# Column matmuls, an earlier load of the state-space inputs, and the tap transposes behind the small vectors' copy

## The chip, the cores and the metric

The kernel runs on one core of one Trainium2 chip. The metric is the device time of one execution in microseconds (us), as the median of several runs. Engines are named as in the profile: PE is TensorE's matmul side, PEld its weight loads, DVE is VectorE, ACT is ScalarE, POOL is GpSimd, SP is SyncE (here it only issues DMAs).

## The reference

Two residual layers over 256 tokens of width 1024, all float32. Each layer computes six conditioning vectors from one vector `c`, and uses them as shift, scale and gate of its two sub-layers:

```
mod = (c_act @ w_mod[l] + b_mod[l])        # 6 * 1024 values, six vectors
sh1, sc1, g1, sh2, sc2, g2 = split(mod, 6)
h = rmsnorm(x, norm1_g[l]) * (1 + sc1) + sh1
proj = h @ w_in[l]                          # q k v | conv a b | ssm u | gates
mixed = gate_a * attention + gate_c * conv + gate_s * ssm
x = x + g1 * (mixed @ w_out[l])
h2 = rmsnorm(x, norm2_g[l]) * (1 + sc2) + sh2
x = x + g2 * ((silu(gate) * up) @ w_ffn_out[l])
```

The state-space (ssm) branch needs small tables made from `ssm_b_*` (2 x 128 KB a layer) and `ssm_c_*` (2 x 128 KB a layer). The convolution branch needs 31 taps for each of 512 channels.

## The kernel before, in words

Every large weight block is 1 MB and goes through one of four buffers `raw`. SP loads it; ACT rounds it to a high part `whi` (line 1018); DVE subtracts to get the low part `wlo` (line 1363); PE then runs three matmuls for each product (lines 547 to 549: high x high, high x low, low x high). The blocks follow one fixed list of names: `su` 0 and 1, `q` 0 and 1, `kv`, and so on, then the gates, `wo`, and at the end of a layer the feed-forward blocks `fg`, `fu`, `fo`. Each engine runs its own program in that order, so an engine that waits holds up all that stands behind it in its program. Small work (rotations, attention, ssm, convolution) is set between the blocks at numbered places.

The conditioning product runs beside the blocks in pieces `mod` (line 583), three groups `ng` of 2048 values a layer, so six groups in all. The sum lies in PSUM bank `b_mod` as four rows, at partitions 0, 32, 64 and 96, of 512 values each; the other partitions hold copies and unused rows. DVE adds the bias into `modrow` (line 1517, 128 x 512). PE then brings the values into columns in `mod_columns` (line 591): it transposes all of `modrow` in four pieces of 128 x 128, and DVE copies out the 16 columns that matter with a stride (`mod_vectors`, line 1505). Group 0 of layer 0 is needed by the first norm (line 1540); the others are made ahead, among the blocks.

SP's program is the list `ITEMS` of `mod` and `main` blocks, each with a wait until its `raw` buffer is free, with other loads set between. `load_c` issues the two `ssm_c` loads into `uc` (line 441), `load_b` the two `ssm_b` loads into `yc` (line 437). In layer 0 they stand before the block `("main", 0, 2)`, which is `q` 0; `("main", 0, 1)` is `su` 1. The users of `uc` are a POOL copy (line 988) and then the transposes of `prep_round` on PE (line 769); the user of `yc` is `b_source` on DVE (line 1456).

The small per-channel vectors of a layer (norm gains, biases, ssm parameters) land as rows in `prod` and are transposed by PE into bank `b_y` (`small_columns`, lines 869 and 870); DVE copies them to `vec` and `ldv` (lines 1761 and 1762), whose end is the semaphore `vec_cp`. The taps are transposed into other columns of the same bank (`tap_columns`, line 879) and copied to `tapv` (line 1767). For layer 1 both happen in layer 0 between the blocks `fg` 0 and `fu` 0.

Of the kernel before, what the change touches and what calls it, by code (L numbers as in the profile page):

```python
# [30 lines left out]
P = 128  # L31
# [150 lines left out]
def lo_engine(i):  # L182

    return "dve"
# [70 lines left out]
def trunk(nc, A, out):  # L255
    with ExitStack() as ctx:
        def sb(name, shape, dt=F32):
            return ctx.enter_context(nc.sbuf_tensor(name, shape, dt))

        def sem(name):  # L260
            return ctx.enter_context(nc.semaphore(name))

        bank = [ctx.enter_context(nc.psum_tensor(f"bank{n}", [P, 512], F32)) for n in range(8)]
        b_mod, b_y = bank[2], bank[3]
# [38 lines left out]
        modrow = sb("modrow", [P, 512])  # L303
# [3 lines left out]
        ident = sb("ident", [P, P])  # L307
        ones = sb("ones", [P, P])
        rot = sb("rot", [P, P])
        consts = sb("consts", [P, 16])  # L310
# [10 lines left out]
        modv = sb("modv", [P, 48])  # L321
# [40 lines left out]
        b_ready, cc_ready, c_twice, tap_tr, tap_cp = sem("b_ready"), sem("cc_ready"), sem("c_twice"), sem("tap_tr"), sem("tap_cp")  # L362
# [8 lines left out]
        ldt_spread, vec_tr, vec_cp, c_tr, silu_c, c_ready = (  # L371
            sem(n) for n in "ldt_spread vec_tr vec_cp c_tr silu_c c_ready".split())
        row_zero, s_bias, mod_row, mod_tr, mod_ready, scale_ready, g_tr, g_ready = (
            sem(n) for n in "row_zero bias_landed mod_row mod_tr mod_ready scale_ready g_tr g_ready".split())
# [28 lines left out]
        def landed_in(item):  # L403

            return raw[SLOT[item]][:, :], s_land[SLOT[item]], LANDED[item]
# [17 lines left out]
        def small_vectors(eng, l):  # L423

            for r0, n, name in ((R_N1, 8, "norm1_g"), (R_N2, 8, "norm2_g"), (R_DWB, 4, "conv_dw_b"),
                                (R_LNG, 4, "conv_ln_g"), (R_LNB, 4, "conv_ln_b"), (R_D, 4, "ssm_d")):
                eng.dma_start(rows[r0:r0 + n, :], A[name][l].rearrange("(r c) -> r c", c=P)).then_inc(s_rows[l], 16)
            for r0, name in ((R_ARE, "ssm_a_re"), (R_AIM, "ssm_a_im")):
                eng.dma_start(rows[r0:r0 + ST, :], A[name][l].rearrange("(s g) n -> s (g n)", g=2)).then_inc(s_rows[l], 16)
            eng.dma_start(ldt[:, :], A["ssm_log_dt"][l].rearrange("(s g) -> s g", g=2)).then_inc(s_rows[l], 16)  # L430

        def load_taps(eng, l):
            eng.dma_start(taps, A["conv_dw_w"][l]).then_inc(s_taps[l], 16)

        def load_b(eng, l):
            for c, name in enumerate(("ssm_b_re", "ssm_b_im")):
                eng.dma_start(bn[:, c], A[name][l].rearrange("g n i -> (g n) i").rearrange("(s p) i -> p s i", p=P)).then_inc(s_b[l], 16)

        def load_c(eng, l):
            for c, name in enumerate(("ssm_c_re", "ssm_c_im")):  # L440
                eng.dma_start(csrc[:, c, :, 0:HEAD], A[name][l].rearrange("g o n -> (g o) n").rearrange("(s p) n -> p s n", p=P)).then_inc(s_cc[l], 16)

        def load_x(eng):
            for j in range(2):
                eng.dma_start(x[:, j, :], A["x"][0, j * P:(j + 1) * P, :]).then_inc(s_x, 16)

        def load_bias(eng, l, ng):
            eng.dma_start(modrow[0:P:32, :],
                          A["b_mod"][l, ng * MODC:(ng + 1) * MODC].rearrange("(q n) -> q n", q=4)).then_inc(s_bias, 16)

        def late_constants(eng):
            eng.dma_start(rot[:, :], A["c_rot"]).then_inc(s_const2, 16)
            eng.dma_start(posi, A["positions"].to_broadcast([P, T])).then_inc(s_const2, 16)
            eng.dma_start(sink[:, :, :], A["attn_sinks"].rearrange("(o l) q -> o l q", o=1).to_broadcast([P, DEPTH, NQ])).then_inc(s_const2, 16)

        @block.sync
        def _(sp):
# [33 lines left out]
            for item in ITEMS:  # L491
                if item == ITEMS[1]:
                    load_x(sp)
                if item == ("main", 0, 2):
                    load_c(sp, 0)
                    load_b(sp, 0)
                if item == ("main", 0, 3):
                    late_constants(sp)
                was = AFTER.get(item)
                if was and was[0] == "main":  # L500

                    e = lo_engine(was[2])
                    sp.wait_ge(s_lo[e], LO_NO[(was[1], was[2])] + 1)
                elif was:

                    sp.wait_ge(s_modused, MOD_NO[was] + 1)
                dst, landed, _ = landed_in(item)
                if item[0] == "mod":
                    _, l, ng, k = item
                    if k == 4 and (l, ng) != (0, 0):  # L510

                        sp.wait_ge(mod_tr, 3 * l + ng)
                        if ng != 1:
                            sp.wait_ge(g_tr, 4 * l + (2 if ng == 2 else 0))
                        load_bias(sp, l, ng)
                    sp.dma_start(dst, A["w_mod"][l, k * P:(k + 1) * P, ng * MODC:(ng + 1) * MODC]).then_inc(landed, 16)
                else:
                    if item[1:] == (0, AT[("gc", 3)]) and DEPTH > 1:

                        sp.wait_ge(gl_read, 4)  # L520
                        small_vectors(sp, 1)
                        load_taps(sp, 1)
                    for d, src in main(item[1], item[2], dst):
                        sp.dma_start(d, src).then_inc(landed, 16)
                    if item[1] == 0 and DEPTH > 1 and item[2] == AT[("fg", 0)]:

                        sp.wait_ge(c_lo, 1)
                        load_c(sp, 1)
                        load_b(sp, 1)
                    if item[1:] == (DEPTH - 1, AT[("fg", 0)]):  # L530

                        sp.wait_ge(s_ready, 2 * DEPTH)
                        sp.dma_start(final_g, A["final_norm_g"].rearrange("(o n) -> o n", o=1).to_broadcast([P, D])).then_inc(s_final_g, 16)
            for n in range(4):
                j, c = divmod(n, 2)
# [7 lines left out]
        def _(pe):  # L543
            mm = nc.tensor.matmul
# [42 lines left out]
            def mod_columns(n):  # L587

                pe.wait_ge(mod_row, n + 1)
                for j in range(4):  # L590
                    last = nc.tensor.transpose(b_mod[:, j * P:(j + 1) * P], modrow[:, j * P:(j + 1) * P], ident[:, :])
                last.then_inc(mod_tr, 1)

            def g_rows(l, ng, half):
# [278 lines left out]
            def tap_columns(l):  # L873

                pe.wait_ge(s_taps[l], 16)
                if l == 0:
                    pe.wait_ge(vec_cp, 1)
                for c in range(CT):
                    last = nc.tensor.transpose(b_y[:, 256 + c * 32:256 + c * 32 + TAPS], taps[:, c * P:(c + 1) * P], ident[0:TAPS, 0:TAPS])
                last.then_inc(tap_tr, 1)  # L880
# [41 lines left out]
            for k in range(DK):  # L922
# [10 lines left out]
                if k == 3:  # L933
                    tap_columns(0)
            mod_columns(0)

            def behind_norm(l, i):
# [395 lines left out]
        def _(dve):  # L1333
            step = Steps(s_dve)
            V = nc.vector
# [164 lines left out]
            def mod_vectors(l, ng):  # L1500

                n = 3 * l + ng
                dve.wait_ge(mod_tr, n + 1)
                c0 = 16 * ng
                V.tensor_copy(modv[:, c0:c0 + 16].rearrange("p (q j) -> p j q", q=4), b_mod[:, :].rearrange("p (j r) -> p j r", j=4)[:, :, 0:P:32]).then_inc(mod_ready, 1)
                dve.wait_ge(mod_ready, n + 1)
                if ng != 1:
                    s, m0, r0 = (scale1, M_SC1, R_N1) if ng == 0 else (scale2, M_SC2, R_N2)
                    V.scalar_tensor_tensor(out=s[:, :], in0=modv[:, m0:m0 + DK], scalar=1.0, in1=vec[l][:, r0:r0 + DK], op0=ALU.add,
                                           op1=ALU.mult).then_inc(scale_ready, 1)  # L1510
                    dve.wait_ge(scale_ready, 2 * l + (ng == 2) + 1)
# [244 lines left out]
            def small_vectors_in(l):  # L1756

                dve.wait_ge(vec_tr, l + 1)
                if l:
                    dve.wait_ge(tap_tr, l + 1)  # L1760
                V.tensor_copy(vec[l][:, :], b_y[:, 0:VROWS])
                V.tensor_copy(ldv[l][:, :], b_y[:, P:P + ST]).then_inc(vec_cp, 1)

# [64 lines left out]
            lo(0)  # L1828
            mod_bias(0)
            mod_vectors(0, 0)  # L1830
            norm(0, "su", 0, scale1, M_SH1)
            lo(1)
            b_source(0, 0)
            for l in range(DEPTH):
                for i in range(NB):
                    for n in mod_ends_at(l, i - 2):
                        mod_vectors(*divmod(n, 3))
# [88 lines left out]
```

## Time and profile before

| what | value |
|---|---|
| three runs | 1014.95, 1015.76 and 1019.72 us; median 1015.76 us |
| profiled execution, its own time | 1014.95 us |
| its span, first to last instruction | 1013.1 us |
| mean granted TensorE clock | 0.972 of full speed |
| PE busy, DVE busy, ACT busy | 937.6, 669.5, 469.1 us |

The profiled execution is the fastest of the three and lies 0.81 us under the median. What lies outside its span is 1.85 us. The granted clock has two levels, 1.00 (2.4 GHz) and 0.50 (1.2 GHz); a value between them in a row is a stretch that holds some of both.

### The profile page before, as it was taken

Reading aid. Unit: us, or ns where it says so; the run is one execution under the profiler, and the core shown is the slowest. Engines: PE = TensorE matmul, PEld = TensorE weight load, DVE = VectorE, ACT = ScalarE, POOL = GpSimd, SP = SyncE. Lnnn points to the kernel's source line nnn. Section 1 sums busy time; section 2 is a strip of 40 time slices with the busy share of each in tenths; the row PEclk is TensorE's granted clock in tenths of the full one; section 3 lists DMA queues with packets and bytes.
Section 4 is the critical chain, followed back from the end, with each engine's and each line's share of the span. In section 5 each row is a group of like instructions: output and inputs, shape, how many; then the busy total and the mean of one; then the engine's idle time right before and its main releaser. Section 6 shows DMA issues by size and latency. Waiting matters only on the chain.

```text
span 1013.1 us, 16086 instructions
## 1 busy us (share of the span) xinstructions
PE 937.6 (93%) x6839; PEld 785.3 (78%) x6839; DVE 669.5 (66%) x913; ACT 469.1 (46%) x548; POOL 9.3 (1%) x11
## 2 busy tenths in 40 slices
PE   5689998999999999999997998999999899999995
PEld 2488885666766979889996997666676699999994
DVE  3773977999477673565456576899966655454445
ACT  4485135623645664545345323574264454343342
POOL 2000000000000000000000000000000000000000
PEclk9799999999999999999998999999999989999998
DMA  9965235548767555565657335454967545565621
GB/s 345 227 214 209 85 126 208 206 133 285 263 246 192 184 180 208 208 209 208 225 191 166 126 126 197 153 207 151 275 231 281 190 133 201 170 204 169 203 87 41
DMA packets 128023, 194.01 MB, mean 192 GB/s; under 512 B 30706, under 2 KB 90618, under 8 KB 121808
## 3 DMA queue, kind: packets, MB, share of 16 engines
q1 hardware_dynamic: 127608, 192.85, 56.9%
q8 instruction: 54, 0.88, 0.4%
q10 hardware_dynamic: 344, 0.14, 0.1%
q14 instruction: 17, 0.14, 0.0%
HBM read 191.93 MB, written 1.05 MB: 190 GB/s over the span
## 4 chain that ended last, share of the span: by engine, by line
PE 64%; DVE 23%; DMA 5%; ACT 4%; issue 3%; ACTq 1%; DVEq 0%
PE bank L547 18%; PE bank L548 18%; PE bank L549 18%; DVE wlo L1363 7%; DVE yc L1648 7%; PE bank L583 2%; DMA prod<-in_conv_dw_w 2%; PE bank L648 2%; ACT whi L1018 1%; PE bank L671 1%; DMA raw<-in_w_in 1%; DMA raw<-in_w_out 1%; PE bank L659 1%; DMA raw<-in_w_mod 1%; PE bank L769 1%
## 5 line engine op out<-in xcount | busy, mean ns | idle before, releaser
L1363 DVE TENSOR_TENSOR wlo<-raw,whi 128x2048 fp32r<-128x2048 f32 (+1 forms) x135 | 302.7, 2243 | 234.7 <-PE bank L549 191.9
L1018 ACT ACTIVATE whi<-raw 128x2048 fp32r<-128x2048 f32 x132 | 252.3, 1912 | 159.7 <-DMA raw<-in_w_in 75.4
L547 PE MATMUL bank<-hhi,whi 128*128 128x256 f32 x992 | 289.3, 292 | 11.8 <-DVE hlo L1545 9.3
L548 PE MATMUL bank<-hlo,whi 128*128 128x256 f32 x992 | 285.2, 287 | 0.0
L549 PE MATMUL bank<-hhi,wlo 128*128 128x256 f32 x992 | 284.8, 287 | 0.0
L547 PEld LDWEIGHTS bank<-hhi,whi 128*128 128x128 f32 x992 | 195.0, 197 | 21.0 <-issue 16.2
L548 PEld LDWEIGHTS bank<-hlo,whi 128*128 128x128 f32 x992 | 195.1, 197 | 0.6
L549 PEld LDWEIGHTS bank<-hhi,wlo 128*128 128x128 f32 x992 | 194.9, 196 | 0.0
L547 PE MATMUL bank<-whi,bhi 128*128 128x512 f32 x304 | 121.4, 399 | 3.4 <-DVE wlo L1363 3.4
L548 PE MATMUL bank<-wlo,bhi 128*128 128x512 f32 x304 | 119.1, 392 | 0.0
L549 PE MATMUL bank<-whi,blo 128*128 128x512 f32 x304 | 118.7, 391 | 0.0
L547 PE MATMUL bank<-whi,hhi 128*128 128x512 f32 x256 | 105.5, 412 | 2.4 <-DVE wlo L1363 2.2
L549 PE MATMUL bank<-whi,hlo 128*128 128x512 f32 x256 | 100.4, 392 | 0.0
L548 PE MATMUL bank<-wlo,hhi 128*128 128x512 f32 x256 | 100.4, 392 | 0.0
L1648 DVE SCALAR_TENSOR_TENSOR yc<-uc,tapv,yc 128x256 f32<-128x256 f32 x240 | 97.3, 479 | 0.1
L547 PEld LDWEIGHTS bank<-whi,bhi 128*128 128x128 f32 x304 | 57.4, 189 | 21.3 <-issue 5.3
L1238 ACT ACTIVATE bhi<-gate 128x512 fp32r<-128x512 f32 x22 | 13.9, 632 | 124.5 <-DVE gate L1722 124.5
L547 PEld LDWEIGHTS bank<-whi,hhi 128*128 128x128 f32 x256 | 48.4, 189 | 26.0 <-issue 11.7
L583 PE MATMUL bank<-raw,cact 128*32 128x512 f32 x384 | 54.9, 650 | 13.8 <-DMA raw<-in_w_mod 9.5
L549 PEld LDWEIGHTS bank<-whi,blo 128*128 128x128 f32 x304 | 57.3, 189 | 12.5
L548 PEld LDWEIGHTS bank<-wlo,bhi 128*128 128x128 f32 x304 | 57.5, 189 | 10.6
L549 PEld LDWEIGHTS bank<-whi,hlo 128*128 128x128 f32 x256 | 48.3, 189 | 10.7
(250 smaller groups left out, 818.0 us busy)
## 6 DMA issues: line engine op xcount, KB each, us to landing
raw<-in_w_mod SPq DMA_DIRECT2D x48, 1024.0 KB, 7.2
raw<-in_w_ffn_in SPq DMA_DIRECT2D x44, 1024.0 KB, 5.1
raw<-in_w_in SPq DMA_DIRECT2D x38, 1024.0 KB, 5.3
raw<-in_w_ffn_out SPq DMA_DIRECT2D x22, 1024.0 KB, 5.0
raw<-in_w_out SPq DMA_DIRECT2D x8, 1024.0 KB, 6.1
raw<-in_w_in SPq DMA_DIRECT2D x16, 256.0 KB, 4.9
raw<-in_ssm_glu_b SPq DMA_DIRECT2D x4, 1024.0 KB, 5.1
raw<-in_ssm_glu_a SPq DMA_DIRECT2D x4, 1024.0 KB, 5.1
```

The source lines that it names most:

```text
L547: mm(o, w_hi, a_hi, start=start, stop=False, skip_group_check=True)
L548: mm(o, w_hi, a_lo, start=False, stop=False, skip_group_check=True)
L549: return mm(o, w_lo, a_hi, start=False, stop=stop, skip_group_check=True)
L583: last = mm(b_mod[32 * q:32 * q + 32, :], cact32[:, k, :], weights[:, q * 512:(q + 1) * 512], start=(k == 0), stop=(k == DK - 1), skip_gro ...
L648: last = mm(o, bl[r, a, STEPS - 1 - j, k, :], u_ssm[r, k, j * NC:(j + 1) * NC], start=(k == 0 and a == 0 and j == 0), stop=(j == STEPS - 1 ...
L659: mm(o[:, t * NC:T], kf[:, k, t, :], u_ssm[:, k, 0:(STEPS - t) * NC], start=(k % 2 == 0 and t == 0), stop=False, skip_group_check=True)
L671: last = mm(b_out[k // 2][r:r + 32, c0 + 1:c0 + NC], ca[:, a, j, 4 * k + 2 * half + q, :], s[:, a, q, k, 0:NC - 1], start=False, stop=(a = ...
L769: last = nc.tensor.transpose(round_bank(l, n)[:, k * P:(k + 1) * P], src, ident[:, :])
L1018: fn(whi[mi % N_HI][:, :], raw[SLOT[item]][:, :], ACT.Copy).then_inc(s_hi, 1)
L1238: fn(bhi[:, a:a + 2, :], gate[:, a:a + 2, :], ACT.Copy).then_inc(act_hi, 1)
L1363: part = V.tensor_tensor(wlo[mi % N_LO][:, n], raw[SLOT[("main", *divmod(mi, NB))]][:, n], whi[mi % N_HI][:, n].bitcast(F32), ALU.subtract)
L1648: last = V.scalar_tensor_tensor(out=yc[:, c, :], in0=uc[:, c, k:k + T], scalar=w, in1=yc[:, c, :], op0=ALU.mult, op1=ALU.add)
```

## The change

It has three parts.

1. In layer 0, SP issues the two `ssm_c` and the two `ssm_b` loads one block earlier: before `su` 1, no longer before `q` 0.
2. `mod_columns` no longer transposes `modrow`. Each of its four pieces is the stationary operand of a float32 matmul whose moving operand is `consts[:, 0:4]`, four columns that hold a 1 at partition 0, 32, 64 or 96. Each gives 128 x 4 values, side by side in the first 16 columns of `b_mod`, and DVE copies these 16.
3. In layer 1's tap transposes, PE first waits for DVE's copy of the small vectors (`vec_cp`, as layer 0's do already), and DVE's copy no longer waits for the tap transposes (`tap_tr`).

```
-                if item == ("main", 0, 2):
+                if item == ("main", 0, 1):
                     load_c(sp, 0)
                     load_b(sp, 0)
...
                 for j in range(4):
-                    last = nc.tensor.transpose(b_mod[:, j * P:(j + 1) * P], modrow[:, j * P:(j + 1) * P], ident[:, :])
+                    last = mm(b_mod[:, 4 * j:4 * j + 4], modrow[:, j * P:(j + 1) * P], consts[:, 0:4], start=(j == 0), stop=(j == 3), skip_group_check=True)
                 last.then_inc(mod_tr, 1)
...
                 pe.wait_ge(s_taps[l], 16)
-                if l == 0:
-                    pe.wait_ge(vec_cp, 1)
+                pe.wait_ge(vec_cp, l + 1)
...
-                V.tensor_copy(modv[:, c0:c0 + 16].rearrange("p (q j) -> p j q", q=4), b_mod[:, :].rearrange("p (j r) -> p j r", j=4)[:, :, 0:P:32]).then_inc(mod_ready, 1)
+                V.tensor_copy(modv[:, c0:c0 + 16].rearrange("p (q j) -> p j q", q=4), b_mod[:, 0:16].rearrange("p (j q) -> p j q", q=4)).then_inc(mod_ready, 1)
...
                 dve.wait_ge(vec_tr, l + 1)
-                if l:
-                    dve.wait_ge(tap_tr, l + 1)
                 V.tensor_copy(vec[l][:, :], b_y[:, 0:VROWS])
```

## Rows read from the trace of the kernel before

**Rows 1.** The page: busy time by engine, and the chain's shares.

```profile
PE 937.6 (93%) x6839; PEld 785.3 (78%) x6839; DVE 669.5 (66%) x913; ACT 469.1 (46%) x548; POOL 9.3 (1%) x11
...
PE 64%; DVE 23%; DMA 5%; ACT 4%; issue 3%; ACTq 1%; DVEq 0%
```

**Rows 2.** The chain, 36 to 48 us: start, length, what.

```profile
36.45 1.13 PE bank L591 x4
...
40.63 1.80 ACT whi L1018
...
44.94 2.20 DVE wlo L1363
47.14 1.14 DVE gate L1456
```

**Rows 3.** Timeline of SP's DMA issues, 22 to 40 us: start, length.

```profile
26.45 0.38 SPq L524 DMA_DIRECT2D raw<-in_w_in  x1
...
27.50 3.76 SPq L441 DMA_DIRECT2D uc<-in_ssm_c_im  x1
...
33.71 3.46 SPq L437 DMA_DIRECT2D yc<-in_ssm_b_im  x1
```

**Rows 4.** Tile raw, issues at 26 to 27 us; tile yc, 20 to 60 us.

```profile
DMA to landing us min/median/max: 10.2/10.2/10.2
...
DMA to landing us min/median/max: 6.3/6.6/6.9
```

**Rows 5.** Timeline of POOL, ACT and PE, the loads' users, 37 to 49 us.

```profile
37.37 0.61 POOL L988 COPY uc<-uc 128x512 f32<-128x512 f32 x1 [12.44 <-DMA uc<-in_ssm_c_im]
...
45.66 1.92 ACT L1018 ACTIVATE whi<-raw 128x2048 fp32r<-128x2048 f32 x1 [1.37 <-DMA raw<-in_w_in]
...
47.77 1.03 PE L769 MATMUL bank<-ident,uc 128*128 128x128 f32 x8
```

**Rows 6.** Timeline of PE, PEld and DVE: column transposes, and loads before short matmuls.

```profile
36.45 1.11 PE L591 MATMUL bank<-ident,modrow 128*128 128x128 f32 x4 [0.89 <-DVE modrow L1517]
37.60 0.19 DVE L1505 COPY modv<-bank 128x16 f32<-128x16 f32 x1 [1.21 <-PE bank L591]
...
84.05 0.16 PEld L782 LDWEIGHTS bank<-prod,decay 128*32 128x32 f32 x7
...
122.91 0.42 PEld L659 LDWEIGHTS bank<-u_ssm,kf 128*128 128x128 f32 x3
```

**Rows 7.** Line 659 by shape: count | busy us, mean ns | idle.

```profile
L659 PEld LDWEIGHTS bank<-u_ssm,kf 128*128 128x128 f32 x64 | 9.5, 191 | 0.5
```

**Rows 8.** The chain at two later groups.

```profile
206.05 0.48 DVE yc L1648
...
304.88 0.44 PE bank L591 x4
```

**Rows 9.** Timeline of DVE, PE and PEld, 332 to 339 us.

```profile
332.04 2.29 DVE L1363 TENSOR_TENSOR wlo<-raw,whi 128x2048 fp32r<-128x2048 f32 x1 [1.78 <-PE bank L549]
332.12 0.32 PEld L879 LDWEIGHTS bank<-ident,prod 31*128 31x128 f32 x4
332.48 0.39 PE L547 MATMUL bank<-hhi,whi 128*128 128x256 f32 x1
...
334.38 0.16 DVE L1762 COPY ldv<-bank 128x16 f32<-128x16 f32 x1
...
338.60 2.29 DVE L1363 TENSOR_TENSOR wlo<-raw,whi 128x2048 fp32r<-128x2048 f32 x1 [3.86 <-PE bank L549]
```

**Rows 10.** Windows of PE: length, busy (count), granted clock, DMA share, GB/s.

```profile
60.00:66.00 6.00, 4.67 (x27) 0.72 0.53 184
324.00:330.00 6.00, 4.33 (x34) 1.00 1.10 377
```

**Rows 11.** Waits of PE, 59 to 61.5 us and 323 to 326 us: total, times, longest.

```profile
PE bank L769 <- ACT blx L1082: 2.1, 1, 2.1
...
PE bank L547 <- DVE hlo L1545: 2.3, 1, 2.3
```

## The prediction

> **What bounds the kernel now.** I read the page first: PE is busy for 93% of the span, and the chain that ended last is 64% PE and 23% DVE [rows 1]. A microsecond of PE is therefore worth a microsecond only where the chain runs on PE, and each edit has to be placed in the chain first. I then read the chain piece by piece around each edited line, the timeline of the engines there, and the windows with the granted clock.
>
> The first norm is where part 1 and part 2 meet. The chain goes from the landing of the last `mod` weights over the four column transposes to DVE's norm, then through ACT's rounding of `su` 1 at 40.63, DVE's `wlo` at 44.94 and `b_source` at 47.14 [rows 2]. Here PE is no bound; the queue of ACT and DVE is.
>
> **Part 1, the earlier loads.** Who waits for `ssm_c` and `ssm_b`? POOL's copy starts at 37.37, as `ssm_c` lands, but PE uses its result only at 47.77 [rows 5]. The second `ssm_b` load was issued at 33.71 and landed 6.3 to 6.9 us later [rows 3, 4], so by 40.6 at the latest, while DVE comes to it at 47.14 straight from its own work [rows 2]. Nobody on the chain waits for either, so landing earlier gains nothing. One load behind them gains: `q` 0 is waited for by ACT, 1.37 us until 45.66 [rows 5], but the chain between 44.94 and 50 runs on DVE, so this is worth nothing as well.
>
> What it costs is the load that is moved past. `su` 1 is issued at 26.45 and lands 10.2 us later, at 36.7 [rows 3, 4]; ACT takes it up at about 40.6 [rows 2], so it has 3.9 us of slack. After the change it stands behind four issues that took SP from 26.87 to 37.17 [rows 3]. They can start about 1.2 us earlier, since SP need not wait for `su` 1's buffer first, which puts the issue of `su` 1 at about 36.0. The two long issue times look like SP waiting for room in the queue (the one of 3.76 us ends at 31.3, that of 3.46 at 37.2, where 0.38 us do for a 1 MB load), and with `su` 1 no longer ahead of them the room may come sooner; 34.5 is the early end. A 1 MB load in a queue with nothing ahead takes about 5 us: estimate of the landing 39.5 to 41.2. ACT wants it at 40.6, or 0.85 later by part 2. So the price is 0, with 0.6 us as the upper end if part 2 turns out free. I take 0.
>
> **Part 2, the columns.** Before: four transposes. After: four float32 matmuls with the same stationary 128 x 128 and 4 moving columns in place of 128. A float32 matmul that is no transpose has two loads and two matmuls in the trace (line 659 has 64 loads in two layers for 32 calls [rows 7]), a transpose one of each. So 4 loads become 8, while the moving part shrinks to nothing.
>
> What does a load cost when nothing long covers it? The nearest row is that of float32 loads 128 x 128 ahead of 64-column matmuls: three of them take 0.42 us, the last one 0.19, so they start 0.115 apart; I use 0.11 [rows 6]. Eight of them: 0.88 us. The four transposes take 0.44 us of the chain at full clock [rows 8]. That is +0.44 us of PE for each group. The bounds: the 32-column loads that go into different quarters of the array start about 0.01 to 0.02 apart (seven in 0.16 us, the last 0.11 of it) [rows 6]; at that price a group would gain 0.3 us. If loads and matmuls didn't overlap at all, 8 x 0.16 = 1.3 us, +0.85. I take the 128 x 128 row, which is the same shape and type.
>
> The Trainium skill ("TensorE: Matmul & The Clock Gate", Back-to-back issue gap) gives an isolated matmul of 1 to 64 columns a floor of about 25 ns; eight of them would be 0.2 us, and a group would then gain 0.24 us. The row of line 659 speaks against it, since there the load and not the matmul sets the pace.
>
> Now the six groups one by one. The first one runs at the granted clock of 0.50 and is wholly on the chain: the copy starts 1.15 us after the first transpose [rows 6]. At half clock the loads start 0.22 apart: 8 x 0.22 = 1.76, and the last short matmul ends about 0.21 later (a transposed 128-column piece lasts 0.42 there, of which 0.21 is streaming). Copy after 2.0 us: +0.85. The groups at 205 and 691 us lie where the chain is DVE's convolution [rows 8]: 0. Those at 304.9, 495.0 and 791.1 lie on PE's chain, with the same row three times [rows 8]: 3 x 0.44 = +1.32. DVE's copy reads 16 values a partition either way: 0. Sum of part 2: +2.2 us, between -1.6 and +4.
>
> **Part 3, the taps of layer 1.** DVE's dropped wait is worth nothing: its copies come at 334.25, directly behind the `wlo` that it started at 332.04, and the tap transposes were over by 332.5 [rows 9]. The new wait of PE is another matter. PE finishes `fg` 0 at 331.9, does the small transposes, goes on to the taps at 332.12 and begins `fu` 0 at 332.48. The copy that it now waits for ends at 334.54 [rows 9], since DVE does 2.29 us of `wlo` first. PE would then start the tap transposes at 334.60 and `fu` 0 0.36 us later, at 334.96: 2.48 us late. What stands behind it in PE's queue is the block `fu` 0, and DVE waits for its end: 3.86 us idle until 338.60 [rows 9]. There is no slack on that side, ACT waits in turn for DVE, and SP's loads hang on DVE; so the whole 2.48 us goes into the end. Bounds 2.3 and 2.6. POOL's clearing of `prod` comes later too and has no one waiting.
>
> **The clock behind that stall.** PE will do nothing but four tiny transposes between 332.1 and 335.0. After the wait of 2.13 us that ended at 61.33 the granted clock fell to its lower level and came back: 0.72 over the 6 us from 60, so 1.7 us lost [rows 10, 11]. After the wait of 2.3 us that ended at 325.67 it stayed 1.00 [rows 10, 11]. Both happen after stalls of this length. Mine is a little longer than both, so I take the drop as somewhat likelier than not: +1.7 us, bound below 0, above 3.4 (two such stretches).
>
> **The sum.** 0 + 2.2 + 2.5 + 1.7 = +6.4 us on the profiled execution's own 1014.95 us: 1021.3 us, 0.63% more. Without the clock drop it is +4.7, 1019.6 us, 0.46%. The median of the runs shown is 0.8 us above that execution, and one run of three was 4.8 us above it. The measurement of this kernel tells about 0.5%, 5 us, from no change, so the two cases lie on either side of that line.
>
> **The rivals.**
> *The clock stays up.* The same sum without the drop: the stall falls as the one at 325 did. 1019.6 us, within 0.5%. This is the mechanism that puts the result on the other side; its place is the stretch from 335 to 339 us, and it decides from 1.3 us on (6.4 - 5.1). For it speaks the window from 324, against it that from 60 [rows 10].
> *The matmul sets the pace, not the load.* Then a group costs no more than before, or gains 0.24 to 0.3 us on the chain three times and 0.5 at the start. Sum -1.3 + 2.5, and +1.7 with the drop: 1016.2 to 1017.9 us; at price nothing 1017.4 to 1019.1. The Trainium skill's floor of 25 ns, on the page named above, would lead here. Against it stands the spacing of 0.11.
> *`su` 1 comes late.* If the four small loads hold SP up for longer than before, `su` 1 lands at 43 or 44, ACT's queue with the second half of the norm stands behind it, and 2 to 3 us come on top: 1022 to 1024.5 us. Against it: those four issues took 10.3 us in all while 3 MB were queued ahead, and now less is.
> *PE's stall is taken up later*, by a wait that shrinks. It would need a releaser that doesn't hang on `fu` 0, which I find none of up to 362 us. 1018 us.
>
> **How the numbers follow.** Forecast with the drop 0.38; the clock stays up 0.27; the matmul sets the pace 0.15, half of it with the drop; `su` 1 late 0.10; taken up 0.05; something else that makes it faster 0.05. The range 1016.5 to 1024.0 takes in all but the outermost of them. Slower by over 0.5%: the forecast mostly, the late `su` 1 and a fifth of the rival without the drop, 0.49; faster 0.04; within, the rest, 0.47.
>
> **What would show each step.** Right: two PE records for each of four calls at line 591, eight loads about 0.11 apart at full clock and 0.22 at the start, and the first copy of `modv` 2.0 us after the first of them; a wait of PE at line 879 of about 2.4 us, released by DVE's line 1762, and `fu` 0 about 2.5 us later behind `fg` 0's end; a clock under 1.00 right behind it. ACT's rounding of `su` 1 without a wait for a DMA. Wrong: loads closer than 0.08 at line 591; ACT idle for `in_w_in` before its second rounding; no PE wait at line 879, or PE's later waits shorter by as much. The total would go wrong most easily by the clock's drops elsewhere, each worth 1.7 to 3.4 us, which a shift of a microsecond can add or take away.

## The result, and the profile after

| | before | after |
|---|---|---|
| median of 6 executions each, side by side on one chip | 1018.59 us (1014.95 to 1020.23) | 1025.16 us (1022.23 to 1026.0) |
| ratio, with its 95% interval | | 1.007 [1.0051, 1.0091] |
| profiled execution, its span | 1014.95, 1013.1 us | 1024.41, 1022.6 us |
| mean granted clock in it | 0.972 | 0.966 |

The changed kernel is slower by 0.7% by the ratio, by 6.6 us (0.64%) by the medians, where the forecast's sum was 6.4 us. The forecast time of 1021.3 us was still missed, and so was its range's upper end of 1024.0, since the kernel before itself has a median of 1018.59 us in this comparison and the sum stood on an execution of 1014.95. Three of the six executions of the kernel before are those that the prediction had; the three new ones took 1018.01, 1019.16 and 1020.23 us. Of all executions in this document one, of e1_loads, was in a slow state (1323.99 us at a mean clock of 0.65) and is left out of its median and ratio.

Of the page after, busy time and the chain's shares, which answer to [rows 1]:

```profile
PE 945.4 (92%) x6863; PEld 792.6 (78%) x6863; DVE 669.6 (65%) x913; ACT 469.1 (46%) x548; POOL 8.7 (1%) x11
...
PE 63%; DVE 23%; DMA 5%; ACT 5%; issue 3%; ACTq 1%; DVEq 0%
```

There are 24 more records on PE, as six groups of eight in place of four need. The other engines work as long as before. In the changed kernel, lines from 876 on stand one lower than before up to about 1500, and three lower behind the dropped wait.

The first norm, timeline after, beside [rows 2, 6]:

```profile
36.18 1.78 PEld L591 LDWEIGHTS bank<-consts,modrow 128*128 128x128 f32 x8 [2.62 <-DVE modrow L1516]
36.18 1.87 PE L591 MATMUL bank<-consts,modrow 128*128 128x4 f32 x8 [0.89 <-DVE modrow L1516]
38.09 0.18 DVE L1504 COPY modv<-bank 128x16 f32<-128x16 f32 x1 [1.96 <-PE bank L591]
```

Eight weight loads (LDWEIGHTS, side PEld) take 1.78 us at the lower clock, 0.22 each, and the copy starts 1.91 us behind the first matmul; it was 1.15. The chain after, at the three groups that lie on PE (each stood at 0.44, one of them in [rows 8]):

```profile
306.43 0.79 PE bank L591 x8
...
502.35 0.79 PE bank L591 x8
...
800.04 0.79 PE bank L591 x8
```

That is +0.35 us each, 0.10 us for one load and matmul. The Trainium skill ("TensorE: Matmul & The Clock Gate", LDWEIGHTS (loading the stationary operand)) gives a load its number of columns divided by 1.2, in ns: 107 ns for 128, an estimate of 0.85 us for eight. The trace roughly agrees at the higher clock, with 0.79; at the lower one it has 1.78, twice that, so the one figure does not hold for both. Its floor of 25 ns for a short matmul (same page, Back-to-back issue gap) is no use here, since the loads set the pace.

SP's issues after, beside [rows 3], and the users of the loads, POOL and ACT, beside [rows 5]:

```profile
25.62 0.43 SPq L441 DMA_DIRECT2D uc<-in_ssm_c_re  x1
26.10 0.51 SPq L441 DMA_DIRECT2D uc<-in_ssm_c_im  x1
26.65 3.47 SPq L437 DMA_DIRECT2D yc<-in_ssm_b_re  x1
30.16 3.72 SPq L437 DMA_DIRECT2D yc<-in_ssm_b_im  x1
33.93 7.34 SPq L524 DMA_DIRECT2D raw<-in_w_in  x5
```

```profile
34.10 0.61 POOL L987 COPY uc<-uc 128x512 f32<-128x512 f32 x1 [8.82 <-DMA uc<-in_ssm_c_im]
```

```profile
41.02 1.89 ACT L1017 ACTIVATE whi<-raw 128x2048 fp32r<-128x2048 f32 x1
```

`su` 1 is issued at 33.93, 7.5 us later than before, lands 6.5 us on, at 40.4, and ACT rounds it at 41.02 without having waited for it. `ssm_c` is there 3.3 us earlier for POOL, and nothing comes of that.

The taps, timeline after of PE and then of DVE, beside [rows 9]:

```profile
334.87 0.28 PE L549 MATMUL bank<-hhi,wlo 128*128 128x256 f32 x1
...
337.91 0.60 PE L878 MATMUL bank<-ident,prod 31*128 31x31 f32 x4 [2.40 <-DVE ldv L1759]
338.44 0.58 PE L547 MATMUL bank<-hhi,whi 128*128 128x256 f32 x1
```

```profile
335.26 2.29 DVE L1362 TENSOR_TENSOR wlo<-raw,whi 128x2048 fp32r<-128x2048 f32 x1 [2.99 <-PE bank L549]
337.47 0.21 DVE L1758 COPY vec<-bank 128x64 f32<-128x64 f32 x1
337.60 0.16 DVE L1759 COPY ldv<-bank 128x16 f32<-128x16 f32 x1
338.55 0.29 DVE L1764 COPY tapv<-bank 128x124 f32<-128x124 f32 x1 [0.79 <-PE bank L878]
345.79 2.29 DVE L1362 TENSOR_TENSOR wlo<-raw,whi 128x2048 fp32r<-128x2048 f32 x1 [6.96 <-PE bank L549]
```

PE waits 2.40 us for two small copies that stand behind DVE's `wlo` of 2.29 us. From one `wlo` to the next it was 6.56 us (332.04 to 338.60), and it is now 10.53: +3.97. The windows after show what is not the wait itself. Their columns are the length, the busy time (and count) of PE, PEld, DVE, ACT and POOL, the granted clock, the DMA share and GB/s; all windows below have the same:

```profile
336.00:338.00 2.00, 0.09 (x1) 0.12 (x2) 1.76 (x3) 1.58 (x1) 0.00 (x0) 0.96 0.00 0
338.00:340.00 2.00, 2.00 (x11) 1.94 (x12) 0.29 (x1) 0.00 (x0) 1.36 (x2) 0.50 0.57 176
340.00:342.00 2.00, 2.00 (x14) 2.00 (x14) 0.00 (x0) 0.00 (x0) 0.14 (x1) 0.68 1.00 347
```

PE did almost nothing from 336 to 338, and from 338 to 340 the granted clock was at its lower level (0.50, 1.2 GHz), where a 256-column matmul lasts 0.41 us in place of 0.28. The 3.97 us are 2.5 of waiting (e5 below measures it alone) and 1.5 of the clock.

### The profile page after: what moved, and what is told of

The parts are those of the page before. It is cut to its first block, busy times and chain, and to the rows that moved or that the text cites. A ratio compares the mean times of both kernels' runs of the same rounds, so it can differ in the third digit from the quotient of the medians.

```text
span 1022.6 us, 16134 instructions
## 1 busy us (share of the span) xinstructions
PE 945.4 (92%) x6863; PEld 792.6 (78%) x6863; DVE 669.6 (65%) x913; ACT 469.1 (46%) x548; POOL 8.7 (1%) x11
## 3 DMA queue, kind: packets, MB, share of 16 engines
HBM read 191.93 MB, written 1.05 MB: 189 GB/s over the span
## 4 chain that ended last, share of the span: by engine, by line
PE 63%; DVE 23%; DMA 5%; ACT 5%; issue 3%; ACTq 1%; DVEq 0%
PE bank L547 18%; PE bank L548 17%; PE bank L549 17%; DVE wlo L1362 7%; DVE yc L1647 7%; PE bank L583 2%; DMA prod<-in_conv_dw_w 2%; PE bank L648 2%; ACT whi L1017 2%; DMA raw<-in_w_in 2%; PE bank L671 1%; DMA raw<-in_w_out 1%; PE bank L659 1%; DMA raw<-in_w_mod 1%; PE bank L747 1%
## 6 DMA issues: line engine op xcount, KB each, us to landing
raw<-in_w_mod SPq DMA_DIRECT2D x48, 1024.0 KB, 7.2
raw<-in_w_ffn_in SPq DMA_DIRECT2D x44, 1024.0 KB, 5.1
raw<-in_w_in SPq DMA_DIRECT2D x38, 1024.0 KB, 5.5
raw<-in_w_ffn_out SPq DMA_DIRECT2D x22, 1024.0 KB, 5.0
raw<-in_w_out SPq DMA_DIRECT2D x8, 1024.0 KB, 6.2
raw<-in_ssm_glu_b SPq DMA_DIRECT2D x4, 1024.0 KB, 5.1
raw<-in_ssm_glu_a SPq DMA_DIRECT2D x4, 1024.0 KB, 5.1
```

## The experiments

Each ratio is to the kernel before, run beside it on the same chip, with a 95% interval. e8 has one execution, the profiled one.

**One part at a time.** Four kernels made from the one before: part 1 alone, part 2 alone, part 3 alone, and parts 1 and 2 together (each with its lines of the diff shown above).

e1_loads, the first hunk alone. 

> Part 1 alone: the four ssm loads of layer 0 one block earlier. My reading (nobody on the chain waits for them, and su 1 still lands before ACT takes it up): 0 us, ratio 0.9995 to 1.0005 apart from the scatter of the runs. If the loads are what gains or costs: the rival 'su 1 late' wants +2 to +3 us, ratio 1.002 to 1.003, with ACT idle for in_w_in ahead of its second rounding; a gain would need b_source or the transposes of ssm_c to start earlier.

e2_columns, the second and fourth hunk alone. 

> Part 2 alone: column matmuls in place of the transposes. Loads set the pace: +0.76 us at the first group (as the changed kernel shows) and +0.44 at each of the three groups on PE's chain, together +2.1 us, ratio 1.002; PE records at line 591 start 0.11 apart at full clock. The matmul sets the pace (the rival): the groups at full clock gain 0.24 to 0.3 us each, sum -0.1 us, ratio 1.000.

e3_taps, the third and fifth hunk alone. 

> Part 3 alone: layer 1's tap transposes wait for DVE's copy. The stall goes into the end in full: +2.5 us, and +1.7 us more in the executions where the clock falls behind it, so +2.5 to +4.2 us, ratio 1.0025 to 1.0041. The rival that the stall is taken up later: under +1 us, ratio under 1.001, with the same delay seen at fu 0 and gone at the end of layer 0.

e4_no_taps, the first, second and fourth. 

> Parts 1 and 2 without part 3. If the parts add up: +2.1 us, ratio 1.002, that is the changed kernel less 2.5 to 4.2 us. If part 3 isn't the larger part of the loss, this is near the changed kernel, ratio 1.005 or more.

| kernel | median, beside a before of 1014.64 us | ratio |
|---|---|---|
| e1_loads | 1013.93 | 1.000 [0.9986, 1.0014] |
| e2_columns | 1016.95 | 1.0022 [1.0003, 1.0041] |
| e3_taps | 1018.5 | 1.0045 [1.0027, 1.0063] |
| e4_no_taps | 1016.66 | 1.0023 [1.0004, 1.0041] |

The parts add up: 0 + 0.22 + 0.45 = 0.67%, where the whole change has 0.7. The earlier loads are worth nothing alone and nothing on top of part 2. Each interval is some 0.2% wide to either side, so the sum is good to no more than that. Part 3 alone costs more in its own trace than in the changed kernel's; its windows say why:

```profile
334.00:337.00 3.00, 3.00 (x15) 2.94 (x16) 0.29 (x1) 0.00 (x0) 1.51 (x2) 0.50 0.77 242
337.00:340.00 3.00, 3.00 (x16) 3.00 (x15) 0.00 (x0) 0.00 (x0) 0.00 (x0) 0.50 0.31 108
```

The wait is again 2.4 us, but the clock stays low for all of these 6 us. From `wlo` to `wlo` it is 11.95 us here (331.32 to 343.27), +5.39: 2.5 of waiting and 2.9 of the clock. The whole kernel has only 3.9 us more in its median, so an execution does not always lose that much.

**The stall with the clock held.** Part 3, with five matmuls of no use (their result is overwritten) between `fg` 0's end and the wait:

```
+                if l:
+                    for n in range(5):
+                        mm(bank[4 + n % 4][:, 0:T], ones[:, :], x[:, 0, 0:T], start=True, stop=True, skip_group_check=True)
                 pe.wait_ge(vec_cp, l + 1)
```

e5_taps_filled. 

> Part 3 alone, but PE runs five float32 matmuls of 256 columns, whose result nobody reads, on the bank that fo 0 clears later, in front of the wait for DVE's copy (2.15 us at 0.43 each). This separates the stall from the clock: the wait for the copy stays, but PE isn't idle. If the clock behind the stall is the rest of part 3's 4.6 us: the clock stays at 1.00 behind it, fu 0 is 2.5 us late and no more, +2.5 us, ratio 1.0025. If the 4.6 us have another cause, for instance DVE's changed order: ratio 1.0045 as before. If DVE's copy itself comes later, more.

Measured: 1018.23 us beside 1016.2, ratio 1.0016 [1.0004, 1.0027]. The timeline of its PE and DVE:

```profile
334.00 2.43 PE L878 MATMUL bank<-x,ones 128*128 128x256 f32 x10
336.38 0.43 PE L881 MATMUL bank<-ident,prod 31*128 31x31 f32 x4
```

```profile
333.82 2.29 DVE L1365 TENSOR_TENSOR wlo<-raw,whi 128x2048 fp32r<-128x2048 f32 x1 [2.99 <-PE bank L549]
...
342.87 2.29 DVE L1365 TENSOR_TENSOR wlo<-raw,whi 128x2048 fp32r<-128x2048 f32 x1 [5.73 <-PE bank L549]
```

The filler takes the place of the wait (0.35 us of which is left), so `fu` 0 is as late as the wait alone would make it: from `wlo` to `wlo` 9.05 us, +2.49, the wait's own length. The clock is 1.00 all through, and nothing else is lost:

```profile
334.00:337.00 3.00, 3.00 (x17) 2.40 (x17) 2.48 (x4) 2.15 (x2) 0.06 (x1) 1.00 0.08 31
337.00:340.00 3.00, 3.00 (x27) 3.00 (x27) 0.14 (x1) 0.00 (x0) 1.45 (x2) 1.00 0.89 290
```

Against e3, 0.29% or 2.9 us is gone, as much as the clock took in e3's trace. So the stall's price has two terms, the wait and the clock behind it. The traces show both; the ratios fit, but the shifts below move a ratio by as much, so they alone would not show it.

**The stall taken away.** Part 3, with the tap transposes and their copy one block later on both engines, when `vec_cp` is long done:

```
                         small_columns(l + 1)
-                        tap_columns(l + 1)
+                    if i == PREP_AT and l + 1 < DEPTH:
+                        tap_columns(l + 1)
```

e6_taps_later. 

> Part 3 alone, with layer 1's tap transposes and their copy set one block later (ahead of fg 1, not fu 0), where DVE's copy of the small vectors is long done. If the wait for the copy is the whole cost: fu 0 follows fg 0 without a stall, ratio 1.000 (within 0.0015). If anything else of part 3 costs: up to 1.0045.

Measured: 1016.95 us beside 1016.2, 0.9998 [0.9982, 1.0013]. DVE's timeline:

```profile
334.68 2.29 DVE L1363 TENSOR_TENSOR wlo<-raw,whi 128x2048 fp32r<-128x2048 f32 x1 [2.99 <-PE bank L549]
...
340.99 2.29 DVE L1363 TENSOR_TENSOR wlo<-raw,whi 128x2048 fp32r<-128x2048 f32 x1 [3.81 <-PE bank L549]
```

6.31 us from `wlo` to `wlo` (without the tap transposes, which now come later), and no cost. The order of the waits is harmless; what costs is where the wait stands in PE's queue.

**Load or matmul?** The kernel before, with float32 matmuls of 64 moving columns in place of its transposes (DVE's copy takes the 16 columns out with a stride, as before):

```
+                    last = mm(b_mod[:, 64 * j:64 * j + 64], modrow[:, j * P:(j + 1) * P], ident[:, 0:P:2], start=(j == 0), stop=(j == 3), skip_group_check=True)
```

e8_columns64. 

> The kernel before with column matmuls of 64 moving columns (every second column of the identity) in place of 4. Loads set the pace: the eight records of a group start 0.11 apart at full clock as with 4 columns, and a group on PE's chain costs the same 0.88 us. The matmul sets the pace: with 64 columns a group takes clearly longer than with 4, by up to 8 x 0.05 = 0.4 us.

Measured: 1019.62 us, one execution. Its chain at the same three groups, all alike:

```profile
306.40 0.84 PE bank L591 x8
```

Sixteen times the columns of part 2 (0.79) add 0.05 us to eight matmuls, so the moving columns don't set the pace; what stays is the load.

**A shift alone.** The clock drops at different places in each of these traces, so I asked what a mere shift does. The kernel before, with tiny transposes of `crow` in PE's first wait, while it waits for the first loads; nothing of theirs is used:

```
+            for _ in range(30):
+                nc.tensor.transpose(b_y[:, 0:DK], crow[:, :], ident[0:DK, 0:DK])
             for k in range(DK):
                 mod_block(0, 0, k)
```

e12_shifted. 

> The kernel before with 30 transposes of c's 8 rows, nobody's input, in PE's first wait (3.8 to 8.1 us), which covers them. They add as many PE instructions as the fillers of the start do (60 records) and touch neither a wait nor the clock of any later stretch. If the place of the instructions in PE's program costs by itself (PE's waits that the trace calls issue grow or new ones come, 1.9 us at 95 us before, 2.3 to 2.7 us in the kernels with more PE instructions): ratio 1.001 to 1.004, and issue waits of 1 to 2.7 us at other places. If the fillers' loss has another cause: 1.000.

Measured: 1020.94 us beside 1016.7, 1.0048 [1.0031, 1.0065]. That is as much as part 3 has, with no wait and no work added on any path. Four others follow it: 10 and 60 in the kernel before, and 10 and 30 in the changed kernel.

e14_shift10. 

> The kernel before with 10 tiny transposes of crow in PE's first wait (20 more records on PE's side), nothing else. Theory A (the position of PE's instructions sets where its waits for nothing visible fall, and what they cost): another set of such waits than with 30, and a ratio anywhere between 0.998 and 1.006. Theory B (a time rises with the number of added instructions, 60 records for +0.48%): +0.16%, ratio 1.0016. Theory C (run e12 fell by chance into another state of the clock): ratio 1.000.

e15_shift60. 

> The same with 60 tiny transposes (120 more records). They may reach past PE's first wait by at most 1 us at its start. Theory A: a ratio between 0.998 and 1.006 without relation to the count. Theory B: +0.96%, ratio 1.0096. Theory C: 1.000 to 1.001.

e16_after10. 

> The changed kernel with 10 tiny transposes in PE's first wait. If its +0.7% is all its own waits and loads (0.76 us at the start, 3 x 0.35, 2.5 of the stall and the clock behind it, 5.8 in sum), ratio 1.0055 to 1.009 as before. If the position of instructions has a share in it, the ratio moves by up to 0.4% either way: 1.003 to 1.011.

e17_after30. 

> The changed kernel with 30 tiny transposes in PE's first wait. If the shift's +0.48% of the kernel before is a price that adds, ratio 1.0115. If it is a matter of position, anywhere from 1.003 to 1.011. If the changed kernel's cost is its own and the shift costs nothing here, 1.007.

| transposes added | kernel before | changed kernel |
|---|---|---|
| 0 | 1 | 1.007 [1.0051, 1.0091] |
| 10 | 1.0013 [1.0001, 1.0025] | 1.011 [1.0092, 1.0129] |
| 30 | 1.0048 [1.0031, 1.0065] | 1.0074 [1.0057, 1.0091] |
| 60 | 1.0059 [1.0041, 1.0077] | not run |

A price that adds for each instruction would put 60 at 1.0096 and the changed kernel with 30 at 1.012; both lie outside the intervals. What is left is that something which depends on the position of PE's instructions matters, by up to 0.6% in the kernel before and 0.4% in the changed one. One place shows how it may. It is a wait of PE for nothing that the profile sees ("issue"). All of them in the view of PE's waits, over the whole execution, first before, then e12:

```profile
PE bank L648 <- issue: 1.9, 1, 1.9
```

```profile
PE bank L648 <- issue: 2.7, 1, 2.7
PE bank L547 <- issue: 2.1, 1, 2.1
PE bank L548 <- issue: 0.8, 1, 0.8
```

The second is new, stands in the middle of a block at 471 us, and the lower clock follows it, as the windows of e12 and then of before show:

```profile
470.00:472.50 2.50, 1.01 (x9) 0.81 (x7) 0.00 (x0) 2.36 (x2) 0.00 (x0) 1.00 0.97 376
472.50:476.00 3.50, 2.87 (x16) 2.88 (x17) 0.00 (x0) 0.00 (x0) 0.00 (x0) 0.68 0.11 36
```

```profile
470.00:472.50 2.50, 2.50 (x18) 2.28 (x18) 0.98 (x1) 0.00 (x0) 0.00 (x0) 1.00 0.17 66
472.50:476.00 3.50, 3.50 (x17) 2.91 (x16) 2.80 (x4) 1.55 (x2) 0.00 (x0) 1.00 0.21 58
```

In e15 a wait of 2.1 us of that kind stands at line 549, in e14 only the one at line 648 has grown, to 2.8. Two executions of one kernel, e9 and e13 below, have nearly the same such waits (2.5 and 0.6 us, 2.4 and 0.4), so they seem to belong to the program. That PE's instructions come too late there is my guess; no run tells what the engine waits for.

The clock is another matter. The changed kernel and the one before have the same wait of PE for ACT, here in the timeline of each, before and then after:

```profile
417.06 0.63 PE L769 MATMUL bank<-ident,ca 128*128 128x128 f32 x4 [2.15 <-ACT blx L1082]
```

```profile
422.78 0.71 PE L769 MATMUL bank<-ident,ca 128*128 128x128 f32 x4 [2.15 <-ACT blx L1081]
```

Windows of 5 us ahead of the end of that wait and behind it, again before and then after:

```profile
412.00:417.00 5.00, 2.92 (x14) 2.08 (x12) 0.53 (x1) 4.85 (x5) 0.00 (x0) 1.00 0.65 261
417.00:422.00 5.00, 4.94 (x31) 4.46 (x32) 3.19 (x4) 2.60 (x3) 0.00 (x0) 1.00 0.42 128
```

```profile
417.70:422.70 5.00, 2.94 (x14) 2.10 (x12) 0.51 (x1) 4.87 (x5) 0.00 (x0) 1.00 0.66 265
422.70:427.70 5.00, 4.92 (x17) 4.05 (x18) 3.07 (x3) 2.58 (x3) 0.00 (x0) 0.66 0.39 126
```

Up to the end of the wait PE does the same work in the same pattern, 14 matmuls in 2.9 us of 5; behind it the clock is 1.00 in one kernel and 0.66 in the other, 1.7 us lost (0.34 x 5). It comes 5.7 us later in the changed kernel, but that is not what decides. e9 and e13 below are one kernel, profiled twice. Each has the same wait (2.14 us, at 412.60 and 413.81), and behind it the windows of e9 and then of e13 are:

```profile
412.54:417.54 5.00, 4.94 (x18) 4.02 (x19) 3.06 (x3) 2.60 (x3) 0.00 (x0) 0.66 0.41 129
```

```profile
413.75:418.75 5.00, 4.94 (x31) 4.49 (x32) 3.19 (x4) 2.61 (x3) 0.00 (x0) 1.00 0.40 127
```

So the same wait of the same program costs a stretch of low clock in one execution and none in another. Over the 18 traces it does in 8, and their times do not sort them: with the wait's end at 418.00 us (e6) the clock stays up, at 418.11 (e4) it falls, at 418.46 (e14) it stays up. The wait of 2.33 us for `hlo`, after which the clock stayed up in [rows 10, 11], is such another: of the 15 traces that have it unfilled, the clock fell behind it in 10, e1's among them (0.58 over 6 us), which has no change near it. A single trace therefore doesn't say whether a wait of this length will cost its clock, and the difference between two traces is in part the luck of the execution.

**Filling waits on purpose.** If a low clock costs, keeping PE busy in its unavoidable waits should pay. The kernel before, with matmuls of no use ahead of a block whose input is late: e9 at the start, before the first ssm rounds and around the norms of both layers; e10 at the start and before those rounds alone; e11 around the norms alone. e9 and e10 also have one more wait of PE at the start, for the copy of the taps (`tap_cp`), since these fillers write where the taps lie.

```
+            def fill(o, n, src):
+                for _ in range(n):
+                    mm(o, ones[:, :], src, start=True, stop=True, skip_group_check=True)
...
                     o = unit_bank(l, i)
+                    fill(o[:, 0:T], 5 if l or kind == "fg" else 3, cosr[:, :] if l or kind == "fg" else x[:, 0, 0:T])
...
+                if k >= 5:
+                    fill(b_y[:, 0:T], {5: 8, 6: 2, 7: 1}[k], x[:, 0, 0:T])
```

e9_fill. 

> The kernel before, with matmuls that nobody reads in PE's waits: eleven among the first mod pieces, four before the transposes at 61 us, three to five before the norm's first product, five among the transposes of the second layer's first norm. If the granted clock falls because of PE's waits and its fall is on the chain: the first group's work and the stretches behind 61, 543 and 809 us run at the higher clock, -5 to -8 us, ratio 0.992 to 0.995. If the lower clock there lies beside other work, or the fillers get in the way: 0.998 to 1.002.

e10_fill_start. 

> Only the fillers of the first 62 us: eleven matmuls among the last three mod pieces of layer 0's first group, four before the transposes at 61 us. If the clock at the start is what the filled kernel gains by: the first group's last piece and its transposes run at 1.00 (about -1.5 us up to the first norm) and the stretch behind 61 us too (-1.5 us), ratio about 0.997. If it is all in the later norms: 1.000.

e11_fill_norms. 

> Only the fillers before the first product of each norm (three in the first, five in the others) and the five among the transposes of the second layer's first norm. The stretches behind 543 and 809 us stay at 1.00: 6.8 us at half speed each in the kernel before, of which 3.4 us each would be lost, if all of it were on the chain. Ratio 0.995 to 0.998. With the start alone as the cause: 1.000.

e13_fill_again, e9's kernel again, on another occasion. 

> The filled kernel once more, beside other kernels and on whatever chip comes. Its two halves alone gave 1.0029 and 0.9978, together 0.9943. If 0.9943 stands it is within 0.992 to 0.996 again; if its halves simply add up, it is near 1.0007.

| kernel | median, and before beside it | ratio |
|---|---|---|
| e9_fill | 1010.94, 1016.2 | 0.9943 [0.9926, 0.996] |
| e13_fill_again | 1010.29, 1016.7 | 0.994 [0.9918, 0.9962] |
| e10_fill_start | 1020.74, 1017.04 | 1.0029 [1.0013, 1.0045] |
| e11_fill_norms | 1015.59, 1017.04 | 0.9978 [0.9959, 0.9998] |

All fillers together beat both kernels, twice. Windows of e9, then of before, at the start:

```profile
26.00:36.00 10.00, 8.51 (x47) 4.87 (x44) 4.86 (x13) 2.95 (x3) 0.00 (x0) 1.00 1.02 314
36.00:60.00 24.00, 20.57 (x153) 18.89 (x152) 22.18 (x32) 18.86 (x27) 0.61 (x1) 1.00 1.01 241
```

```profile
26.00:36.00 10.00, 4.10 (x20) 0.36 (x16) 4.68 (x14) 3.11 (x3) 0.00 (x0) 0.75 0.99 312
36.00:60.00 24.00, 19.77 (x140) 18.99 (x140) 21.20 (x29) 17.44 (x25) 0.61 (x1) 0.82 0.92 233
```

The halves do not add up: e10 is slower. One place where it gives back is the stretch from 92 us, with before under it:

```profile
92.00:106.00 14.00, 11.50 (x149) 11.38 (x150) 4.19 (x7) 1.91 (x1) 0.00 (x0) 0.53 0.37 143
```

```profile
92.00:106.00 14.00, 12.08 (x244) 11.83 (x240) 4.57 (x9) 2.48 (x2) 0.00 (x0) 0.76 0.60 223
```

A clock of 0.53 in place of 0.76 for 14 us is 3.2 us of full speed (0.23 x 14). This is one execution of each, and such a stretch differs between executions too (0.76 in e9, 0.88 in e13). The medians do say that e10 is slower and e9 faster, beyond their intervals; why e10 loses is open, position among the candidates. Of e9's 0.6%, the part that belongs to the fillers themselves stays open by as much as the shifts above are worth.

## Why the prediction was wrong, point by point

**The failing step** is the first sentence of the sum: "0 + 2.2 + 2.5 + 1.7 = +6.4 us on the profiled execution's own 1014.95 us: 1021.3 us". The difference held, the level under it didn't. The six executions of the kernel before that stood beside the changed one have a median of 1018.59 us, 3.6 us above that anchor; on it the same sum gives 1025.0 us, against 1025.16 measured. The prediction said that one run of three was 4.8 us above the anchor, and then let the range's upper end, 1024.0, follow from the rivals' prices alone. The lowest of three executions is not the level of the next ones. Beside the other experiments the kernel before had medians from 1014.64 to 1017.04, so the level itself is uncertain by some 4 us.

**Part 1: 0, right.** e1 measures 1.000. The estimate of `su` 1's issue (34.5 to 36.0) was a little late, 33.93; it landed at 40.4, in the estimated range, and ACT was ready for it only at 41.02. The long issues stayed long: 3.47 and 3.72 us for `ssm_b` re and im, where before `ssm_c` im had 3.76, `ssm_b` re 2.37 and `ssm_b` im 3.46. With `su` 1 no longer ahead, SP is held up one load later, and the four take 8.3 us in place of 10.3 (25.62 to 33.88). Room did come sooner. The rival of a late `su` 1 is out in the trace and by e1.

**Part 2: +2.2, the mechanism right, each term a little large.** At the start +0.76 against +0.85, on PE's chain 3 x 0.35 against 3 x 0.44, so 1.8 us in all. The groups under DVE's convolution have no piece at line 591 in the chain, as said. e2 and e4 measure 2.2 and 2.3 thousandths, but a shift of 10 transposes alone has 1.3, so their size confirms nothing finer than the sign. The rival in which the matmul sets the pace is out: e8, with 16 times the columns, has 0.84 against 0.79.

**Part 3, the wait: +2.5, right.** 2.40 us at line 878, released by the copy, and with the clock held (e5) the step from `wlo` to `wlo` is longer by 2.49. No later wait took it up: from the `wlo` behind the stall to the last one it is 649.02 us in e3's trace (343.27 to 992.29) and 649.33 in e1's (340.43 to 989.76), which has no stall. e3's +3.9 us in the whole time fits, and that rival is out too. e6 shows, to within 0.2%, that the cost is the wait's place alone.

**The clock behind it: +1.7, right in the changed kernel (1.5), 2.9 in e3, bounds 0 and 3.4 kept.** The rival in which the clock stays up, which had 0.27, did not come in any trace where PE is left idle: in e3, the changed kernel and the two shifted ones a window behind the stall has 0.50 to 0.53, and the step from `wlo` to `wlo` is 11.95, 10.53, 10.57 and 11.87 us. Four of four is not proof that it always falls. The row that spoke for this rival, 1.00 behind the wait at 325 us, was the rarer case of its own wait (5 of 15 traces). e5 is that rival made on purpose, and has 1.0016.

**What the prediction didn't have** is the price of position. Trace terms add up to 0.76 + 1.05 + 3.97 = 5.8 us, the measurement says 6.6. At 10 added transposes the changed kernel stands 0.97% above the shifted one before, at 30 it is 0.26% (1.0074 - 1.0048), with none 0.7%. Their mean, 0.64% or 6.5 us, is near the sum, but any one of them could have been what was timed, so that 6.4 and 6.6 agree this closely is in part luck. By its last sentence the prediction saw that the clock's drops elsewhere can come and go; it laid this to a shift of a microsecond, where e9 and e13 show that it needs none, and it put no width on it. The pair of profiled executions has them both ways, and no edit stands beside them: against the changed kernel are the drops behind the waits at 325 and at 417 us of the kernel before, 1.2 us (0.20 x 6) and 1.7; for it is the wait at 61 us, behind which the kernel before had 0.72 [rows 10] and the changed one has 1.00, 1.5 us by the `wlo` at 74 us.

```profile
60.50:66.50 6.00, 4.70 (x41) 4.66 (x42) 3.25 (x10) 5.79 (x10) 0.00 (x0) 1.00 0.54 178
```

**How far that goes.** Shown: the miss of the level, the wait's price, the clock's share of it in the traces at hand, the load's pace, the nothing of part 1. Argued only: that the 0.8 us between 5.8 and 6.6 is position or the executions' own clock. Open: why the kernel before was slower in this comparison than in the later ones, what the "issue" waits wait for, what makes the clock fall behind a wait in one execution and not in the next, and the split of part 2's 0.22%.

## What to carry to other kernels

Before a wait is moved in a queue, look at what the engine that must answer has in hand: here two copies of 0.4 us in all stood behind one of 2.29, so that a wait looking free cost 2.5 us and the clock's fall another 1.5 to 2.9; one block later the same wait is free. A small matmul is priced by its load, and a float32 matmul that isn't a transpose has two. And where differences under 1% are in question, add the difference to a median of several executions, profile a kernel more than once before a drop of the clock is laid to an edit, and vary the position of the instructions before a cause is believed: a run with useless instructions in a wait tells what a mere shift is worth.

## What the runs showed of the hardware that was not expected

- 30 tiny transposes in a wait at the start, off every path, make the kernel slower by 0.48%, and 60 by 0.59%; in the changed kernel 30 leave 0.7% at 0.74%. With 30, a new wait of PE of 2.1 us for nothing visible comes in the middle of a block.
- Of waits of PE of 2.1 to 2.4 us some are followed by the lower clock and some are not, and the same wait in two executions of one kernel, with the same work ahead of it, does either (0.66 in e9, 1.00 in e13, behind 2.14 us).
- Matmuls of no use in waits that exist anyway raised the mean clock from 0.972 to 0.985 and 0.986 and made the kernel faster by 0.6%, on two occasions, while the same fillers at the start alone made it slower by 0.29%.
- Issuing 128 KB can hold SP up for longer than issuing 1 MB: behind `su` 1, which took 0.38 us, the four small loads took 0.58, 3.76, 2.37 and 3.46 us; ahead of it 0.43, 0.51, 3.47 and 3.72, and in e1 0.44, 0.51, 4.54 and 3.90. The hold begins one load later when the 1 MB load isn't ahead.
